# Last down projection of a two-layer diffusion backbone: its gated weight tiles in two buffers of their own, the first two loaded and multiplied in the first up steps

## What is computed

```python
def swiglu(h, w_in, w_out):
    g, u = jnp.split(h @ w_in, 2, axis=-1)
    return (jax.nn.silu(g) * u) @ w_out
...
        x = x + 0.5 * ada_gate(m_lat, 2) * swiglu(ada_in(x, norm_w[l, 2], m_lat, 2), ffn_w_in[l, 1], ffn_w_out[l, 1])
...
    return rms_norm(x, final_norm_w)
```

## Time and profile before

| | before |
|---|---|
| runs, median | 2024.98 us |
| profiled execution, its time | 2022.7 us |
| its span | 2021.0 us |
| TensorE busy | 98% |
| VectorE busy | 64% |
| ScalarE busy | 37% |
| chain of waits, on TensorE | 89% |
| chain of waits, gating (L1090) | 1% |
| mean granted TensorE clock | 0.998 |
| HBM read | 272.99 MB |

### The profile page before, as it was taken

The page is one execution under the profiler, slowest core; times in us unless marked ns, Lnnn a source line. Parts: engine busy times, 40 slices in busy tenths (PEclk is TensorE's granted clock), DMA queues, the critical chain, the costliest instruction groups (busy, mean ns, idle before and its releaser), DMA issues.

```text
span 2021.0 us, 27353 instructions
## 1 busy us (share of the span) xinstructions
PE 1983.9 (98%) x10237; PEld 1679.0 (83%) x10237; DVE 1289.4 (64%) x1808; ACT 749.6 (37%) x982; POOL 109.5 (5%) x166
## 2 busy tenths in 40 slices
PE   9999999999999999999999999999999999999997
PEld 7888888886789989888888988888887888888876
DVE  6877677775648875877677743453345642666676
ACT  5321222346544334322222432222235432745543
POOL 1010011000003200100001000000000000000000
PEclk9999999999999999999999999999999999999999
DMA  8555455530210002655555532343234423044543
GB/s 352 180 189 182 163 201 167 188 105 32 99 58 21 1 22 105 208 186 178 177 192 175 171 108 99 100 176 104 72 116 160 152 85 104 32 167 146 189 164 125
DMA packets 51449, 275.30 MB, mean 136 GB/s; under 512 B 6080, under 2 KB 6400, under 8 KB 31648
## 3 DMA queue, kind: packets, MB, share of 16 engines
q1 hardware_dynamic: 31536, 203.71, 29.0%
q0 software_dynamic: 19104, 69.41, 10.5%
q10 hardware_dynamic: 720, 0.95, 0.2%
HBM read 272.99 MB, written 1.05 MB: 136 GB/s over the span
## 4 chain that ended last, share of the span: by engine, by line
PE 89%; DVE 5%; ACT 4%; issue 2%; DMA 0%; ACTq 0%; SPq 0%
PE ps L1156 15%; PE ps L1158 15%; PE ps L1157 15%; PE ps L1168 6%; PE ps L1391 6%; PE ps L1393 6%; PE ps L1392 6%; PE ps L1169 3%; PE ps L2622 2%; PE ps L2623 2%; PE ps L2624 2%; ACT w_hi L489 2%; DVE w_raw L1090 1%; PE ps L2123 1%; PE ps L2135 1%
## 5 line engine op out<-in xcount | busy, mean ns | idle before, releaser
L757 DVE TENSOR_TENSOR w_lo<-w_raw,w_hi 128x2048 fp32r<-128x2048 f32 (+3 forms) x200 | 417.7, 2089 | 208.4 <-ACT w_hi L489 208.2
L1156 PE MATMUL ps<-h_parts,w_lo 128*128 128x512 f32 (+1 forms) x1424 | 536.2, 377 | 2.9 <-DVE h_parts L1028 1.6
L1158 PE MATMUL ps<-h_parts,w_hi 128*128 128x512 f32 (+1 forms) x1424 | 533.8, 375 | 0.0
L1157 PE MATMUL ps<-h_parts,w_hi 128*128 128x512 f32 (+1 forms) x1424 | 533.7, 375 | 0.0
L489 ACT ACTIVATE w_hi<-w_raw 128x2048 fp32r<-128x2048 f32 (+3 forms) x202 | 352.9, 1747 | 453.1 <-PE ps L1393 254.0
L765 DVE SCALAR_TENSOR_TENSOR ada_product<-ada_w,silu_c 128x1024 bf16<-128x1024 f32 x256 | 313.2, 1224 | 20.9 <-DVE ada_product L765 10.3
L1156 PEld LDWEIGHTS ps<-h_parts,w_lo 128*128 128x128 f32 x1424 | 268.1, 188 | 52.8 <-DVE h_parts L1028 1.6
L1158 PEld LDWEIGHTS ps<-h_parts,w_hi 128*128 128x128 f32 x1424 | 268.1, 188 | 48.6
L1157 PEld LDWEIGHTS ps<-h_parts,w_hi 128*128 128x128 f32 x1424 | 268.1, 188 | 47.3
L501 ACT ACTIVATE sil<-ps 128x512 f32<-128x512 f32 x66 | 39.5, 598 | 481.0 <-PE ps L1158 481.0
L1391 PE MATMUL ps<-hid_parts,w_lo 128*128 128x512 f32 x468 | 182.1, 389 | 0.0
(11 more groups left out here) (365 smaller groups left out, 2554.3 us busy)
## 6 DMA issues: line engine op xcount, KB each, us to landing
w_raw<-in_w_up SPq DMA_DIRECT2D x88, 1024.0 KB, 4.8
ada_w<-in_ada POOLq DMA_DIRECT2D x128, 512.0 KB, 4.0
w_raw<-in_w_down SPq DMA_DIRECT2D x24, 768.0 KB, 4.2
w_raw<-in_w_ret_t SPq DMA_DIRECT2D x16, 1024.0 KB, 4.8
w_raw<-in_w_down SPq DMA_DIRECT2D x24, 640.0 KB, 3.9
w_raw<-in_w_ab SPq DMA_DIRECT2D x14, 1024.0 KB, 4.8
w_raw<-in_w_down SPq DMA_DIRECT2D x11, 1024.0 KB, 4.8
ada<-in_ada SPq DMA_DIRECT2D x8, 1024.0 KB, 21.6
```

Of the source, the lines that this page charges most:

```text
L757: dve.tensor_tensor(w_lo[parts_of(s, slot)][:, 0:elems], w_raw[slot][:, 0:elems], w_hi[parts_of(s, slot)][:, 0:elems].bitcast(F32), ALU.su ...
L1156: pe.matmul(out, lo, rhs_hi(k), start=first and k == 0, stop=False)
L1157: pe.matmul(out, hi, rhs_lo(k), start=False, stop=False)
L1158: mm = pe.matmul(out, hi, rhs_hi(k), start=False, stop=last and k == nk - 1)
```

## The change

Two buffers `gated0` and `gated1`, 8 KB a partition each, take the place where `ada_w` and `silu_c` were. The gated form of `down3` tile t goes to `gated[t % 2]`, and both splits of a `down3` tile read it there. Tiles 0 and 1 are loaded straight into these buffers, after the last `retout` load and a wait for `r_mixed`, and are gated in place behind up steps 0 and 1. Tiles 2 to 10 are loaded to `w_raw` as before and gated from there into the buffer whose tile has just been split: 2 and 3 behind up steps 20 and 21, and each later one, t, behind the split of tile t-2. Their loads wait for `lo_ready` (tiles 2 and 3) or for the gating of the tile two before.

```diff
+    gated = [put(f"gated{i}", [P, 2048], at=at_ada + 8 * KB * i)[0] for i in range(2)]
...
         for name, s0, n, elems, source in runs:
+            if name == "up3":
+                sp.wait_ge(r_mixed, RH)
+                for t in range(2):
+                    sp.dma_start(gated[t][:], a["w_down3"][t]).then_inc(first_rows, 16)
+            if name == "down3":
+                for t in range(2, n):
+                    if t < 4:
+                        sp.wait_ge(lo_ready, s0 + t - 3)
+                    else:
+                        sp.wait_ge(down_gated, t - 1)
+                    sp.dma_start(w_raw[(s0 + t) % 2][:], source(t)).then_inc(raw_ready[(s0 + t) % 2], 16)
+                continue
...
+    def raw_of(s, slot):
+        return gated[(s - S_DOWN3) % 2] if isinstance(s, int) and s >= S_DOWN3 else w_raw[slot]
...
-        act.activation(w_hi[parts_of(s, slot)][:, 0:elems], w_raw[slot][:, 0:elems], ACT.Copy).then_inc(hi_ready, 1)
+        raw = raw_of(s, slot)
+        act.activation(w_hi[parts_of(s, slot)][:, 0:elems], raw[:, 0:elems], ACT.Copy).then_inc(hi_ready, 1)
...
-        dve.tensor_tensor(w_lo[parts_of(s, slot)][:, 0:elems], w_raw[slot][:, 0:elems],
+        dve.tensor_tensor(w_lo[parts_of(s, slot)][:, 0:elems], raw_of(s, slot)[:, 0:elems],
...
-            if cols == LAT and isinstance(r, int) and r >= NF - 3:
-                dve_gate_tile(dve, r - (NF - 3))
+            if cols == LAT and isinstance(r, int) and (r < 2 or r >= NF - 2):
+                dve_gate_tile(dve, r if r < 2 else r - NF + 4)
...
     def dve_gate_tile(dve, t):
-        s = S_DOWN3 + t
+        s, two = S_DOWN3 + t, lambda tile: tile[:].rearrange("p (k n) -> p k n", k=2)
         slot = s % 2
-        raw = w_raw[slot][:].rearrange("p (k n) -> p k n", k=2)
-        dve.wait_ge(raw_ready[slot], 8 * (s - slot) + 16)
-        dve.wait_ge(gate_row_ready, 2)
-        dve.tensor_tensor(raw, raw, over(gate_row[:], 2), ALU.mult).then_inc(down_gated, 1)
+        if t < 2:
+            dve.wait_ge(first_rows, 32)
+            dve.wait_ge(gate_row_ready, 2)
+        else:
+            dve.wait_ge(raw_ready[slot], 8 * (s - slot))
+            dve.wait_ge(lo_ready, s - 1)
+        dve.tensor_tensor(two(gated[t % 2]), two(gated[t] if t < 2 else w_raw[slot]), over(gate_row[:], 2), ALU.mult) \
+           .then_inc(down_gated, 1)
...
             split_lo(dve, s, s % 2, 2048)
-            if r + 3 < NF // 2:
-                dve_gate_tile(dve, r + 3)
+            if r + 4 < NF // 2:
+                dve_gate_tile(dve, r + 4)
```

More of the change, by code:

```diff
@@ L390, in build @@
     gate_spread, gate_row_ready = sem("last_gate_spread"), sem("gate_row_ready")
-    down_gated = sem("down_gated")
+    down_gated, first_rows = sem("down_gated"), sem("first_rows_loaded")
     y_squared, y_floor, y_rooted, y_inverse, y_weighed, y_scaled, y_finished = (
```

## The result

The changed kernel took **2010.61 us**, the median of 4 runs (2009.85 to 2012.05), against 2024.75 us for the kernel before (4 runs). The ratio is 0.9931 with a 95% interval of 0.9914 to 0.9949: faster, by 0.7%, forecast 0.6%. The profiled execution took 2010.45 us, with a span of 2008.7 us.

What follows compares the result with a forecast made beforehand. In `down3` the closed gating-and-split turn fed TensorE every 6.47 us against 5.46 needed, about 14.1 us waiting. Tile 10 12.0 us sooner plus 0.1 at the end gave 12.1 off 2024.98: 2012.8 us, range 2010.7 to 2016.5.

Steps and rivals of the forecast that it cites:

- no wait at all: Lower end of the forecast's range, 2010.7 us: all 14.1 us of TensorE's waiting gone, and 0.1.
- Part 1, the turn opens: `down3`: gating two tiles ahead leaves 4.7 us of work under TensorE's 5.46, so TensorE sets the pace from tile 3.
- Parts 2 to 4: First `down3` tiles: tile 0's wait goes; tile 1 waits 0.1, tile 2 1.0 behind ScalarE's table warming; restarts 0.1 each.
- Part 5, the early gatings: First up steps: gating tiles 0 and 1 costs 0.7 us of wait and 0.1 restart; bounds 0 and 2.2.
- just hidden: Behind up step 0: TensorE could take up tile 3 at 1835.77, up step 2 ends at 1835.78, so no stop.
- Up steps of over 5.55 us to the end: Named sign that the prediction was wrong; the forecast used 5.547 us an up step.
- The low clock: Rival, a `down3` step: TensorE partly at 1.2 GHz now costs 1.7 us, so 2014.5 us; chance 0.12.
- Loads in turn: Rival, entrance to `up3`: loads take 4.8 us each in turn, 7.9 us late, 2020.7 us; chance 0.03.
- The turn closed: Rival, `down3`: ScalarE still meets something once a turn; only 2 to 4 us gained, 2021 to 2023; chance 0.04.
- A lasting low clock: Rival: TensorE stays at 1.2 GHz after new stops, 4.9 us lost per down step, 2029 us and more; chance 0.02.
- Part 6, the loads: Entrance to `up3`: two early loads queue ahead; first `up3` load lands 1804.3, ScalarE takes it 1804.65; cost 0.
- The cover named for this: Entrance to `up3`: VectorE's row update behind that tile's split lets about 1.1 us of load lateness cost next to nothing.

Runs made afterwards that it cites:

- run 1: The changed kernel executed again with no edit: 194.30 us from the first pair of `up3` to the end of the span.
- run 11: The changed kernel again, unedited, timed in 5 rounds beside another kernel on one chip: median 2011.38 us, 194.30 us from the first `up3` pair.
- Run 2: Changed kernel, but from tile 3 on each tile gated behind the split of the tile just before: 202.66 us from first `up3` pair, median 2018.47 us.
- Run 5: Changed kernel with tiles 0 and 1 gated in halves in up steps 2 to 5, square root's table warmed behind tile 3's high part: median 2008.56 us.
- Run 3: Changed kernel, but tiles 0 and 1 loaded to raw slots in their turn and gated behind up steps 19 and 20: 198.30 us from first `up3` pair.
- run 6: Changed kernel with early gatings in halves, plus two unread 2048-column VectorE instructions behind up step 5: 195.58 us from first `up3` pair.
- run 10: Changed kernel with early gatings in halves, plus two unread 1 MB loads behind the early ones: last `retout` to first `up3` pair 12.58 us, not 6.53.
- run 8: Changed kernel, gatings in halves and square root's table warmed later, plus unread 2048- and 256-column VectorE instructions behind up step 5: 191.51 us from first `up3` pair.

## Why the prediction was right

The mechanism was, and nearly each term. Where one was not, another hid it. That the span came out within 0.2 us is luck, and it does not make the size sure: the medians fell by 14.1 us, close to the 14.2 at which the range ended and which stood for no wait at all, while the traces still show waits. The profiled executions give 10.5 us from the first pair of `up3` on, in the first run and in runs 1 and 11 alike; the rest lies ahead of it.

- **Part 1, the turn opens:** tiles 5.44 us apart, forecast 5.46. Run 2 shows that this is 8.4 of the 10.5 us.
- **Parts 2 to 4:** tile 0 begins with the end of the up steps. Tile 1 was forecast with 0.2 us of wait and restart and had 0.18. Tile 2: forecast 1.0 of wait and 0.1 of restart, measured 1.09 - 0.23 = 0.86 and 0.1. Run 5 shows the cause. From the end of the up steps to tile 10 it is 13.2 us less, where the sum had 12.8: 0.15 of the difference lies in the reading 1941.17, which takes the last matmul's length, while the next one follows 0.12 behind its start; the rest in tile 2's wait and in 5.44 for 5.46.
- **Part 5, the early gatings:** 0.8 us of stops forecast, 0.85 measured (distances of 0.48, 0.45, 0.85 and 0.46 us, less four times 0.347). The split behind the first gating, called "just hidden" by 0.01 us, was not; the second stop was smaller in return. A margin of 0.01 us should have been called open.
- **What the sum lacked** is the pace behind those stops, 2.0 us. "Up steps of over 5.55 us to the end" stood in the text as a sign that something was wrong, but no term had it. It is the one miss.
- **Why the span still fitted** (2008.9 forecast, 2008.7 measured): 0.4 us more in the down steps, 0.1 more at the end and the 1.8 us at the front that can't be counted for the change stand against 2.0 us of pace. Counted from the first pair of `up3`, 12.1 were forecast and 10.5 came.
- **The rivals.** The low clock did not come: 1.00 in every stretch after the stops. Run 3 shows it, after waits of 1.6, 2.1 and 2.3 us, at about the price that was said (1.6 us for 1.7); the one stop of 2.46 us in run 6 did not bring it. Loads in turn: shown false by run 10. The turn closed: run 2 is what it would look like. A lasting low clock: not seen; the longest stretch in any trace was 6.8 us, in run 10.

**Part 6, the loads,** was 1.4 us off and cost nothing all the same: the first `up3` load landed when ScalarE began at 1803.91, after 4.34 us of idling. ScalarE's rhythm would have had it there at about 1802.9. So the load was 1.0 us late, where the forecast had it 0.35 us early. The two new loads and this one, with SP's issues (merged, as in the earlier trace rows), landings (medians; the first `up3` load by itself took 7.6 us) and ScalarE's row:

```profile
1791.22 0.82 SPq L420 DMA_DIRECT2D gated<-in_w_down  x2
1796.29 128.62 SPq L433 DMA_DIRECT2D w_raw<-in_w_up  x22
```
```profile
w_raw<-in_w_up SPq DMA_DIRECT2D x4, 1024.0 KB, 5.3
...
gated<-in_w_down SPq DMA_DIRECT2D x2, 1024.0 KB, 8.6
```
```profile
1803.91 1.92 ACT L507 ACTIVATE w_hi<-w_raw 128x2048 fp32r<-128x2048 f32 x1 [4.34 <-DMA w_raw<-in_w_up]
```
The cover named for this held: the row update waited for TensorE's last `retout` pair, 0.55 us before it in both kernels, and from that pair to the first of `up3` are 6.51 us in both. Cost 0, as forecast. Two things made up the 1.4 us. `retout` itself ran faster, at 5.548 us a step here and 5.655 in the kernel before, the same two paces, so ScalarE wanted its tile 0.4 us sooner after the issue of the last `retout` load. And from that issue to the landing of the first `up3` load it was 13.2 us where the forecast had 12.2. Of this 0.8 is that last `retout` load itself, which took 5.6 us here and 4.9 in run 1, where the first `up3` load was only 0.25 us late.

The Trainium skill's figure for loads ("DMA: Bandwidth & Descriptors", section "Where 436 GB/s comes from", about 358 GB/s for a core from HBM) does not hold for these loads: 424 GB/s in the earlier trace rows, 429 in run 10.

## What to carry to other kernels

When an instruction works in place between two others on the same engine, ask for a second buffer before asking for a faster engine: here the work stayed the same, and only the order that the buffer forbade was worth 8 us. Work added to an engine that is not the bound belongs inside its waits, in pieces that fit them; read the gap and the instruction in the same rows. Cost a stop of the bounding engine by what follows it too, and count from the point where the change begins to act, or what varies ahead of it will pass for a gain or hide a loss.

## What the runs showed of the hardware

- **Two paces of TensorE at the same granted clock.** A pair of matmuls (512 and 256 columns) comes every 0.3467 or 0.3533 us. The pace is kept from one stop to the next over 100 us and more. In `up3` it was 0.3467 from the entrance in 13 profiled executions out of 14; the other is run 10, with the long wait and the low clock at the entrance, which had 0.3533 to the end. Behind a stop in `up3` it was 0.3533 in seven of eight executions and 0.3467 in one (run 8); four of the seven are the same two stops of the same up steps. In `retout` it was either, in the changed kernel too, from one execution to the next. Over an up projection of 22 steps the difference is 2.3 us, more than most stops.
- **The same 13 executions put the last up projection's first pair anywhere between 1814.3 and 1817.6 us**, with the same instructions ahead of it but for the loads. The pace in the last 95 pairs of `retout` makes up 0.6 us of this; the rest was not traced to a place. A profile's span alone therefore can't tell 1 or 2 us in this kernel.
